# Backbone kernel: who loads the adaptive tiles, the bank of the context's mean, and where the last adaptive group is computed

## The chip, the cores and the metric

One core of a Trainium2 chip. The metric is device time in microseconds of one execution. Lower is better. The time before is 1668.27 us, the median of three runs (1666.53 to 1669.26).

## The reference, cut to what matters

Two layers over 512 latent tokens (x) and 256 context tokens (ctx) of width 1024, all float32. Layer 0 mixes tokens with a Conformer convolution, layer 1 with retention. Each is followed by a gated FFN of inner width 2816 with a three-tap convolution on the gate, and every sub-layer is modulated by an adaptive vector:

```python
mod_x = (silu_c @ ada_w[i] + ada_b[i])     # 6*1024 columns: shift, scale, gate (mixer); shift, scale, gate (FFN)
mod_c = (silu_cc @ ada_w[i] + ada_b[i])    # the same for the context
hx = modulate(rmsnorm(x, norm1_g[i]), sx1, cx1)
z = hx @ pw1_w + pw1_b                     # conv_module, for x and for ctx
u = dwconv(a * sigmoid(g), dw_w, dw_b)     # 31 taps over the tokens
u = silu(layernorm(u, ln_g, ln_b))         # mean and variance over the 1024 features
x = x + gx1 * (u @ pw2_w + pw2_b)
x = x + gx2 * conv_ffn(modulate(rmsnorm(x, norm2_g[i]), sx2, cx2), ...)
```

In layer 0 the context goes through the same steps with mod_c. The gate gx2 (and gc2) of layer 0 is the last sixth of the adaptive vector, and it is needed only when the FFN's output is added to x.

## The kernel before, in words

Features lie on the 128 partitions, in KT = 8 tiles, tokens along the free axis (LAT = 512, then CTX = 256, TOK = 768). Each engine has a program of its own, and semaphores order them. Every large product is three matmuls over parts rounded to fp32r: ScalarE writes w_hi (split_hi), VectorE w_lo (split_lo), and TensorE multiplies hi by hi, lo by hi and hi by lo. Weights come in units of 128 columns (512 KB) through a ring of RING = 4 buffers. SyncE's load waits until VectorE has split the unit four before (lo_ready).

Order of the stages: a first block (norm, adaptive groups 0 to 3, first units), PW1 with the depthwise convolution block by block, LayerNorm (named norm 1), PW2, FFN0, retention, FFN1, output.

The adaptive vector of layer 0 comes in 12 groups of four tiles of 128 columns. For group m, ada_products(m) streams 2 MB of weights through TensorE against silu(c) and silu(c_ctx), which stand in a 32-column stationary tile, into PSUM bank 6. ada_copy(m) on ScalarE copies the bank, ada_transposes(m) on TensorE transposes it into bank 7, and ada_sum(m) on VectorE adds four partial rows into mod. modulation(...) then adds the bias. SyncE loads groups 5 to 11 (load_group). Groups 10 and 11 lie in PW2.

The adaptive vector of layer 1 is 48 tiles of [128 columns, 1024 features]. GpSimd issues a load per job (L661) into two buffers mod_tile, and VectorE multiplies by the row silu(c) or silu(c_ctx) and sums along the row, one tensor_tensor_reduce per job (mod_jobs, L2160). MOD_JOBS holds 64 jobs, the first 16 tiles twice (c and c_ctx). They are spread over slots 1 to 20 of FFN0. A slot is one pass of VectorE over a feature block; it does some of its jobs ahead of the convolution's taps and the last two behind the products. A load for a buffer waits until the job that used it before is done (mod_job).

The convolution of a block: VectorE forms both_phases and the sum and even taps, TensorE seeds the even taps (first_evens, PSUM bank 4), ScalarE and GpSimd do the odd ones. For the last block TensorE also does ten taps (last_taps, banks 1 and 5), and VectorE ends the rows itself (last_rows). LayerNorm's means are matmuls of conv tiles with the constant matrix mean_of, float32. Two records each stand for one such matmul in the trace. Per tile j there is one for the latents (bank 0) and one for the context (bank 2). TensorE's order there is ada_products(8), first_evens, the mean of tile 0, last_taps, transposes 8, tiles 1 to 6, ada_products(9), tile 7. mu_summed then releases ScalarE and VectorE (center). variance(t) sums the squares of part t (parts 0 and 1 are latents, part 2 the context, 256 tokens each), root and recip make the inverse deviation, and norm_scale, SiLU, norm_hi and norm_lo write H_hi and H_lo of that part.

PW2 runs part by part, four units each. Its first two units of a part go feature by feature (by_rows), each waiting for H_lo of that feature. variance(2) and eight small products (mean_of with itself) follow the second unit of part 1.

Of the kernel before, what the change touches and what calls it, by code (L numbers as in the profile page):

```python
# [29 lines left out]
P = 128  # L30
D = 1024
# [98 lines left out]
MOD_TILES = 48  # L130
MOD_BUFS = 2
MOD_JOBS = [(j, v) for j in range(2 * KT) for v in range(2)] + [(j, 0) for j in range(2 * KT, MOD_TILES)]
# [8 lines left out]
def backbone(nc, x_cols, params, ada_groups, ada_cols, c_rows, w_units, decay_f, decay_b, gn_f, gn_b, eye, ages, tri_low, tri_up, rope_row, rope_col, token_cols, out_cols_major, out):  # L141
    with ExitStack() as stack:
# [158 lines left out]
        sum_part, odd_part = ps[:, 1, 0:HALF], ps[:, 5, 0:HALF]  # L301
# [203 lines left out]

        block = stack.enter_context(nc.Block())
# [12 lines left out]
        def _(sp):  # L519
# [42 lines left out]
            for b in range(KT + 2):  # L562
                load(2 * b + 4, (2 * b + 4) % RING)
                load(2 * b + 5, (2 * b + 5) % RING)
                if b < 6:
                    if b % 2 == 0:
                        load_group(b // 2 + 5)
                else:
                    load_group(b + 2)
            load_ffn(FFN0)  # L570
# [15 lines left out]
        def _(pool):  # L586
# [71 lines left out]
            for n, (j, _) in enumerate(MOD_JOBS):  # L658
                if n >= MOD_BUFS:
                    pool.wait_ge(mod_job, n - MOD_BUFS + 1)  # L660
                pool.dma_start(mod_tile[:, n % MOD_BUFS, :], ada_cols[j]).then_inc(mod_tile_in[n % MOD_BUFS], 16)  # L661
# [18 lines left out]
        def _(pe):  # L680
# [286 lines left out]

            ada_products(8)
            first_evens(PE_EVEN[1], 7 * (KT // 2), 1, S_PW1 // 2 + KT)
            slot_free(S_LN, None)  # L970
            for j in range(KT):
                if j == 1:
                    last_taps(KT - 1)
                    ada_transposes(8)
                if j == KT - 1:
                    ada_products(9)

                pe.wait_ge(conv_ready, j + 1)
                mm(slot(0, 0), mean_of[:], conv[:, j, 0:LAT], j == 0, j == KT - 1)
                m = mm(slot(0, 2)[:, 0:CTX], mean_of[:], conv[:, j, CTX_OUT:OUTW], j == 0, j == KT - 1)  # L980
# [31 lines left out]
            for t in range(3):  # L1012
                for i in range(4):
# [11 lines left out]
                    if n in (3, 5):  # L1025
                        ada_transposes(10 + t)
                    if n == 3:
                        ada_products(11)
# [166 lines left out]
        def _(act):  # L1195
# [171 lines left out]
            A(rstd[:, part(2)], bank(0, 2)[:, 0:PART], ACT.Copy).then_inc(slot_read[1], 1)  # L1367
# [147 lines left out]
            def ln_steps(t, i):  # L1515

                if (t, i) == (1, 0):
                    root(1, 2)
                if t < 2:
                    norm_hi(1, t + 1, LN_TILES[i])  # L1520
                if (t, i) == (0, 3):
                    ada_copy(11)
# [4 lines left out]
            def ffn(blk, s, layer, both, x_at):  # L1527
                f = 0
                for c_no, n in enumerate(CHUNKS):
# [32 lines left out]
                    blk, s = blk + n, s + n  # L1562
                    if c_no < len(CHUNKS) - 1:
                        out_phase(blk, s, x_at, both, layer, 40)
                    elif layer == DEPTH - 1:
                        last_out_phase(blk, s, x_at)
                    else:
                        out_phase_norm(blk, s, x_at, both, layer, 40, 3 + 2 * layer)
# [84 lines left out]
        def _(dve):  # L1653
# [473 lines left out]
            def ln_after(t, i):  # L2127
# [11 lines left out]
                if (t, i) == (1, 1):  # L2139
                    ada_sum(11, 0, 11)  # L2140
                    modulation(11, 0, 40, 48, 12)

            by_parts(2 * PW2, 0, S_PW2, 0, 0, 3, 2, ln_before, ln_after)
            dve.wait_ge(mod_ready, 13)
# [5 lines left out]
            def mod_jobs(slot, early):  # L2150

                first = len(MOD_JOBS) * (slot - 1) // MOD_SLOTS
                end = min(len(MOD_JOBS), len(MOD_JOBS) * slot // MOD_SLOTS)
                cut = max(first, end - MOD_BUFS)
                for n in range(first, cut) if early else range(cut, end):
# [5 lines left out]
                                           accum_out=mod[:, 1, j, c:c + 1]).then_inc(mod_job, 1)  # L2161

            def ffn(blk, s, layer, both, x_at):
# [5 lines left out]
                for c_no, n in enumerate(CHUNKS):  # L2169
                    def pairs(i):  # L2170
                        for q in range(2):
# [28 lines left out]
                            if both and f + 2 * i + q:  # L2200
                                mod_jobs(f + 2 * i + q, False)
                    if both:
# [195 lines left out]
def laid_out(inputs):  # L2398
# [24 lines left out]
    tiles = np.ascontiguousarray(w[1].T).reshape(MOD_TILES, P, D)  # L2423
# [80 lines left out]
```

## Time and profile before

| | |
|---|---|
| median of three runs | 1668.27 us (1666.53 to 1669.26) |
| the profiled execution | 1666.69 us, its span 1664.9 us |
| TensorE busy | 1642.7 us, 99% |
| VectorE busy | 1020.7 us, 61% |
| ScalarE, GpSimd busy | 669.9 us, 199.4 us |
| granted TensorE clock, mean | 0.998 |
| moved by DMA | 175.21 MB |

The span runs from the first to the last instruction. Start times below are us from its start. PE is TensorE, PEld its weight load, DVE VectorE, ACT ScalarE, POOL GpSimd, SP SyncE. L682 is line 682 of the kernel; helpers record all of their calls under one line, so the tiles tell which step a row is: all matmuls stand at L682, transposes of the adaptive groups at L877. A bracket with an arrow names what ended the idle time before the row.

### The profile page before, as it was taken

Reading aid. Unit: us, or ns where it says so; the run is one execution under the profiler, and the core shown is the slowest. Engines: PE = TensorE matmul, PEld = TensorE weight load, DVE = VectorE, ACT = ScalarE, POOL = GpSimd, SP = SyncE. Lnnn points to the kernel's source line nnn. Section 1 sums busy time; section 2 is a strip of 40 time slices with the busy share of each in tenths; the row PEclk is TensorE's granted clock in tenths of the full one; section 3 lists DMA queues with packets and bytes.
Section 4 is the critical chain, followed back from the end, with each engine's and each line's share of the span. In section 5 each row is a group of like instructions: output and inputs, shape, how many; then the busy total and the mean of one; then the engine's idle time right before and its main releaser. Section 6 shows DMA issues by size and latency. Waiting matters only on the chain.

```text
span 1664.9 us, 25492 instructions
## 1 busy us (share of the span) xinstructions
PE 1642.7 (99%) x9978; PEld 1443.8 (87%) x9978; DVE 1020.7 (61%) x1605; ACT 669.9 (40%) x1017; POOL 199.4 (12%) x248
## 2 busy tenths in 40 slices
PE   9999999999999999999999999999999999999998
PEld 7877769998888888888899999999999888888887
DVE  6899987856535652466468665656566644443445
ACT  4655646543322322232344433324235433333333
POOL 1588821011001100001000000000000000000001
PEclk9999999999999999999999999999999999999999
DMA  9322322243425342344213121212112223322321
GB/s 386 133 102 102 138 106 74 64 162 115 154 77 187 141 164 76 101 152 174 79 39 105 52 83 40 81 39 83 51 51 90 89 95 108 101 92 85 101 89 51
DMA packets 46779, 175.21 MB, mean 105 GB/s; under 512 B 5760, under 2 KB 7040, under 8 KB 43616
## 3 DMA queue, kind: packets, MB, share of 16 engines
q1 hardware_dynamic: 34928, 126.38, 22.3%
q0 software_dynamic: 11760, 47.58, 8.3%
q8 instruction: 61, 1.00, 0.3%
q14 instruction: 30, 0.25, 0.0%
HBM read 171.85 MB, written 2.10 MB: 104 GB/s over the span
## 4 chain that ended last, share of the span: by engine, by line
PE 82%; DVE 14%; ACT 3%; issue 1%; DVEq 0%; POOL 0%; ACTq 0%; POOLq 0%
PE ps L682 82%; DVE ps L1844 3%; DVE ps L1862 2%; DVE w_lo L1664 2%; DVE rstd L1670 1%; DVE H_lo L1705 1%; DVE tmp L1693 1%; DVE sq L1693 0%; DVE rstd L1681 0%; ACT sq L1256 0%; DVE X L2021 0%; ACT tmp L1256 0%; ACT H_hi L1247 0%; DVE both_phases L1949 0%; DVE H_lo L1703 0%
## 5 line engine op out<-in xcount | busy, mean ns | idle before, releaser
L682 PE MATMUL ps<-H_hi,w_hi 128*128 128x512 f32 (+1 forms) x1712 | 584.2, 341 | 3.3 <-DVE H_lo L1703 2.2
L682 PE MATMUL ps<-H_lo,w_hi 128*128 128x512 f32 (+1 forms) x1712 | 578.4, 338 | 0.0
L682 PE MATMUL ps<-H_hi,w_lo 128*128 128x512 f32 (+1 forms) x1712 | 577.9, 338 | 0.0
L682 PEld LDWEIGHTS ps<-H_hi,w_hi 128*128 128x128 f32 x1712 | 324.6, 190 | 47.6 <-issue 8.5
L682 PEld LDWEIGHTS ps<-H_lo,w_hi 128*128 128x128 f32 x1712 | 324.6, 190 | 35.3
L682 PEld LDWEIGHTS ps<-H_hi,w_lo 128*128 128x128 f32 x1712 | 324.5, 190 | 35.2
L1664 DVE TENSOR_TENSOR w_lo<-w_raw,w_hi 128x1024 fp32r<-128x1024 f32 x208 | 252.1, 1232 | 99.8 <-ACT w_hi L1209 76.5
L682 PE MATMUL ps<-mid_hi,w_hi 128*128 128x512 f32 (+1 forms) x592 | 200.0, 338 | 0.5
L682 PE MATMUL ps<-mid_hi,w_lo 128*128 128x512 f32 (+1 forms) x592 | 198.7, 336 | 0.0
L682 PE MATMUL ps<-mid_lo,w_hi 128*128 128x512 f32 (+1 forms) x592 | 198.6, 335 | 0.0
L682 PE MATMUL ps<-w_hi,H_hi 128*128 128x256 f32 x512 | 145.1, 283 | 0.2 <-DVE w_lo L1664 0.2
L682 PE MATMUL ps<-w_hi,H_lo 128*128 128x256 f32 x512 | 144.9, 283 | 0.0
L682 PE MATMUL ps<-w_lo,H_hi 128*128 128x256 f32 x512 | 144.8, 283 | 0.0
L1209 ACT ACTIVATE w_hi<-w_raw 128x1024 fp32r<-128x1024 f32 x128 | 132.5, 1050 | 19.0 <-PE ps L682 18.1
L2184 DVE SCALAR_TENSOR_TENSOR tmp<-ps,par,tmp 128x511 f32<-128x511 f32 x66 | 41.6, 658 | 150.8 <-ACT tmp L1543 76.2
L1543 ACT ACTIVATE tmp<-ps,par 128x512 f32<-128x512 f32 x44 | 34.3, 778 | 238.9 <-PE ps L682 238.9
L682 PEld LDWEIGHTS ps<-mid_hi,w_hi 128*128 128x128 f32 x592 | 111.1, 188 | 15.6 <-ACT tmp L1387 2.4
L682 PEld LDWEIGHTS ps<-mid_hi,w_lo 128*128 128x128 f32 x592 | 111.1, 188 | 13.2
L682 PEld LDWEIGHTS ps<-mid_lo,w_hi 128*128 128x128 f32 x592 | 111.2, 188 | 13.1
L617 POOL TENSOR_TENSOR odd_row<-odd_row,prod 128x392 f32<-128x392 f32 x107 | 112.4, 1050 | 43.1 <-ACT prod L1310 29.1
L2016 DVE TENSOR_TENSOR X<-X,tmp 128x768 f32 (+3 forms) x44 | 35.7, 812 | 131.1 <-ACT tmp L1387 131.1
L682 PEld LDWEIGHTS ps<-w_hi,H_hi 128*128 128x128 f32 x512 | 98.2, 192 | 0.7 <-issue 0.4
(285 smaller groups left out, 2202.1 us busy)
## 6 DMA issues: line engine op xcount, KB each, us to landing
w_raw<-in_w_units SPq DMA_DIRECT2D x190, 512.0 KB, 3.6
mod_tile<-in_ada_cols POOLq DMA_DIRECT2D x64, 512.0 KB, 4.9
ada<-in_ada_groups SPq DMA_DIRECT2D x14, 1024.0 KB, 6.5
w_raw<-in_w_units SPq DMA_DIRECT2D x16, 384.0 KB, 4.5
ada<-in_ada_groups POOLq DMA_DIRECT2D x4, 1024.0 KB, 11.0
ada_more<-in_ada_groups POOLq DMA_DIRECT2D x4, 1024.0 KB, 13.8
X<-in_x_cols SPq DMA_DIRECT2D x4, 768.0 KB, 7.0
w_raw<-in_w_units POOLq DMA_DIRECT2D x2, 512.0 KB, 14.6
```

The lines of the kernel that those rows point to most:

```text
L617: nc.gpsimd.tensor_tensor(row, row, prod[:, at % PROD_RING, 0:HALF], ALU.add).then_inc(prod_added, 1)
L682: return nc.tensor.matmul(o, a, b, start=first, stop=last, skip_group_check=True)
L1209: A(w_hi[:, r, :], w_raw[:, r, :], ACT.Copy).then_inc(hi_ready, 1)
L1543: a = A(tmp[:, q, LATS], bank(q, 1), ACT.Identity, scale=w1, bias=b)
L1664: v.tensor_tensor(w_lo[:, r, :], w_raw[:, r, :], w_hi[:, r, :].bitcast(F32), ALU.subtract) \
L1670: v.reciprocal(rstd[:, part(t)], rstd[:, part(t)]).then_inc(rstd_ready, 1)
L1693: o = v.scalar_tensor_tensor(b, X[:, j, part(t)], gain[:, layer, half, j, m:m + 1], rstd[:, part(t)], ALU.mult, ALU.mult)
L1705: o = v.scalar_tensor_tensor(dst, b, shift(norm, t, j), hi, ALU.add, ALU.subtract)
L1844: v.scalar_tensor_tensor(sum_acc, frm, w, sum_acc, ALU.mult, ALU.add).then_inc(tap_done, 1)
L1862: v.scalar_tensor_tensor(even_acc, frm, even_weight(j, b), even_acc, ALU.mult, ALU.add).then_inc(tap_done, 1)
L2016: v.tensor_tensor(row, row, tmp[:, p, 0:w], ALU.add).then_inc(x_updated, 1)
L2184: v.scalar_tensor_tensor(t[:, t0 + 1:t0 + m], b[:, 0:m - 1], wt[0], t[:, t0 + 1:t0 + m], ALU.mult, ALU.add).then_inc(g_taps, 1)
```

## The change

The adaptive group 11 of layer 0 (the FFN's gate, its last four tiles) is no longer computed on TensorE. Its four tiles are put in front of layer 1's 48 as transposed tiles, and each gives two sums, so MOD_JOBS holds 72 jobs. Their results go to the last four tiles of mod of layer 0 (job_sum). load_group(11), ada_products(11), ada_copy(11), the transposes and ada_sum(11) go. modulation over tiles 40 to 48 moves from PW2 into the FFN slot where the eighth job is done, and ScalarE waits for it before the first output phase.

SyncE issues the tile loads: load_first_ffn replaces load_ffn(FFN0), unrolled, and puts the tiles of a slot behind the load of every second unit from the eighth of a chunk on. GpSimd no longer issues any of them.

The context's mean gets bank 5, and the last odd taps bank 2 instead. The context means of tiles 0 to 5 are computed behind ada_products(8), ahead of first_evens; tiles 6 and 7 stay with the latents'.

```diff
@@ constants @@
+GATE_TILES = 4
+MOD_TILES = GATE_TILES + 48
+MOD_PAIRS = GATE_TILES + 2 * KT
+MOD_JOBS = [(j, v) for j in range(MOD_PAIRS) for v in range(2)] + [(j, 0) for j in range(MOD_PAIRS, MOD_TILES)]
-        sum_part, odd_part = ps[:, 1, 0:HALF], ps[:, 5, 0:HALF]
+        sum_part, odd_part = ps[:, 1, 0:HALF], ps[:, 2, 0:HALF]
+        def job_sum(j, c):
+            return mod[:, 0, 48 - GATE_TILES + j, c:c + 1] if j < GATE_TILES else mod[:, 1, j - GATE_TILES, c:c + 1]
+        def jobs_done(slot):
+            return min(len(MOD_JOBS), len(MOD_JOBS) * slot // MOD_SLOTS)
@@ SyncE @@
-                else:
+                elif b <= KT:
                     load_group(b + 2)
-            load_ffn(FFN0)
+            def load_tile(n):
+                if n >= MOD_BUFS:
+                    sp.wait_ge(mod_job, n - MOD_BUFS + 1)
+                sp.dma_start(mod_tile[:, n % MOD_BUFS, :], ada_cols[MOD_JOBS[n][0]]).then_inc(mod_tile_in[n % MOD_BUFS], 16)
+            def load_first_ffn():
+                first, slot, tile = 2 * FFN0, 0, 0
+                for n in CHUNKS:
+                    for u in range(2 * n + KT):
+                        load(first + u, (first + u) % RING, KT if u < 2 * n else n)
+                        if u >= KT and u % 2 == 0 and u < KT + 2 * n:
+                            if slot == 0:
+                                sp.wait_ge(h_lo_ready, KT * PARTS_BEFORE[3])
+                            while tile < min(len(MOD_JOBS), jobs_done(slot) + MOD_BUFS):
+                                load_tile(tile)
+                                tile += 1
+                            slot += 1
+                    first += 2 * n + KT
+            load_first_ffn()
@@ GpSimd @@
-            for n, (j, _) in enumerate(MOD_JOBS):
-                if n >= MOD_BUFS:
-                    pool.wait_ge(mod_job, n - MOD_BUFS + 1)
-                pool.dma_start(mod_tile[:, n % MOD_BUFS, :], ada_cols[j]).then_inc(mod_tile_in[n % MOD_BUFS], 16)
@@ TensorE @@
+            def mean_ctx(j):
+                pe.wait_ge(conv_ready, j + 1)
+                return mm(ps[:, 5, 0:CTX], mean_of[:], conv[:, j, CTX_OUT:OUTW], j == 0, j == KT - 1)
             ada_products(8)
+            pe.wait_ge(sig_ready, KT)
+            for j in range(KT - 2):
+                mean_ctx(j)
             first_evens(PE_EVEN[1], 7 * (KT // 2), 1, S_PW1 // 2 + KT)
...
                 mm(slot(0, 0), mean_of[:], conv[:, j, 0:LAT], j == 0, j == KT - 1)
-                m = mm(slot(0, 2)[:, 0:CTX], mean_of[:], conv[:, j, CTX_OUT:OUTW], j == 0, j == KT - 1)
+                if j >= KT - 2:
+                    m = mean_ctx(j)
...
-                    if n in (3, 5):
-                        ada_transposes(10 + t)
                     if n == 3:
-                        ada_products(11)
+                        ada_transposes(10)
@@ ScalarE @@
-            A(rstd[:, part(2)], bank(0, 2)[:, 0:PART], ACT.Copy).then_inc(slot_read[1], 1)
+            A(rstd[:, part(2)], ps[:, 5, 0:CTX], ACT.Copy).then_inc(slot_read[1], 1)
-                if (t, i) == (0, 3):
-                    ada_copy(11)
+                    if both and c_no == 0:
+                        act.wait_ge(mod_ready, 13)
@@ VectorE @@
-                if (t, i) == (1, 1):
-                    ada_sum(11, 0, 11)
-                    modulation(11, 0, 40, 48, 12)
-            dve.wait_ge(mod_ready, 13)
+            dve.wait_ge(mod_ready, 12)
-                first = len(MOD_JOBS) * (slot - 1) // MOD_SLOTS
-                end = min(len(MOD_JOBS), len(MOD_JOBS) * slot // MOD_SLOTS)
+                first, end = jobs_done(slot - 1), jobs_done(slot)
-                                           accum_out=mod[:, 1, j, c:c + 1]).then_inc(mod_job, 1)
+                                           accum_out=job_sum(j, c)).then_inc(mod_job, 1)
                                 mod_jobs(f + 2 * i + q, False)
+                                if jobs_done(f + 2 * i + q - 1) < 2 * GATE_TILES <= jobs_done(f + 2 * i + q):
+                                    dve.wait_ge(mod_job, 2 * GATE_TILES)
+                                    modulation(10, 0, 40, 48, 12)
@@ host @@
-    tiles = np.ascontiguousarray(w[1].T).reshape(MOD_TILES, P, D)
+    tiles = np.concatenate([w[0][:, (48 - GATE_TILES) * P:].T, w[1].T]).reshape(MOD_TILES, P, D)
```

## Rows read from the trace of the kernel before

**Rows 1.** The page's busy times: us (share of the span) xinstructions, by engine

```profile
PE 1642.7 (99%) x9978; PEld 1443.8 (87%) x9978; DVE 1020.7 (61%) x1605; ACT 669.9 (40%) x1017; POOL 199.4 (12%) x248
```

**Rows 2.** The waits of TensorE, 0 to 420 us: us in total, times, longest us

```profile
PE ps L682 <- DVE sq L1944: 4.5, 3, 2.3
PE ps L682 <- DVE H_lo L1703: 2.2, 2, 2.0
```

**Rows 3.** Timeline of TensorE, 199 to 228 us: start us, us, what xrecords [idle before]

```profile
199.60 1.47 PE L682 MATMUL ps<-ada,silu_c 128*32 128x512 f32 x12
203.42 4.57 PE L682 MATMUL ps<-sq,even_diag 128*128 128x393 f32 x8 [2.35 <-DVE sq L1944]
...
216.14 7.91 PE L682 MATMUL ps<-conv,mean_of 128*128 128x512 f32 x24
223.97 1.92 PE L682 MATMUL ps<-ada,silu_c 128*32 128x512 f32 x16
225.83 1.56 PE L682 MATMUL ps<-conv,mean_of 128*128 128x512 f32 x4
```

**Rows 4.** Timeline of TensorE, the even taps of an earlier block

```profile
161.29 2.88 PE L682 MATMUL ps<-sq,even_diag 128*128 128x393 f32 x8 [1.08 <-DVE sq L1944]
```

**Rows 5.** Busy time of a stretch: length, PE, PEld, DVE, ACT, POOL, granted clock, DMA, GB/s

```profile
204.00:207.40 3.40, 3.40 (x6) 1.69 (x6) 2.25 (x5) 3.40 (x8) 3.11 (x4) 0.50 0.99 417
```

**Rows 6.** Timeline of VectorE, 206 to 233 us

```profile
206.18 0.18 DVE L1722 TENSOR_REDUCE mod<-ps 128x8 f32<-128x32 f32 x1
208.03 0.63 DVE L1908 SCALAR_TENSOR_TENSOR ps<-sq,par,ps 128x393 f32<-128x393 f32 x1 [1.67 <-PE ps L682]
...
221.66 0.57 DVE L1979 TENSOR_TENSOR conv<-tap_sum,odd_row 128x392 f32<-128x392 f32 x1
...
227.42 5.39 DVE L1991 TENSOR_TENSOR conv<-conv,ps 128x256 f32<-128x256 f32 x16 [3.76 <-PE ps L682]
```

**Rows 7.** Timelines of GpSimd (sixth tile) and ScalarE (last gate)

```profile
182.31 1.09 POOL L631 TENSOR_TENSOR conv<-tap_sum,odd_row 128x392 f32<-128x392 f32 x1
...
191.06 0.47 ACT L1326 ACTIVATE rstd<-ps,par 128x256 f32<-128x256 f32 x1
```

**Rows 8.** Busy time of the stretch before PW2, columns as in rows 5

```profile
236.00:239.00 3.00, 1.37 (x16) 0.16 (x8) 0.23 (x1) 2.97 (x6) 0.00 (x0) 1.00 0.00 0
```

**Rows 9.** Timeline of TensorE in PW2, 251 to 277 us

```profile
251.95 1.06 PE L682 MATMUL ps<-ada,silu_c 128*32 128x512 f32 x8
253.95 1.07 PE L682 MATMUL ps<-ada,silu_c 128*32 128x512 f32 x8 [0.94 <-DMA ada<-in_ada_groups]
...
264.26 0.60 PE L877 MATMUL ps<-ident,ada_row 128*128 128x128 f32 x4
...
276.90 0.35 PE L682 MATMUL ps<-H_hi,w_hi 128*128 128x256 f32 x1 [0.19 <-DVE H_lo L1703]
```

**Rows 10.** Timelines of GpSimd and of VectorE in PW2

```profile
259.10 3.05 POOL L642 TENSOR_TENSOR prod<-conv 128x256 f32<-128x256 f32 x4
...
273.67 0.18 DVE L1722 TENSOR_REDUCE mod<-ps 128x8 f32<-128x32 f32 x1
...
274.10 0.42 DVE L1681 TENSOR_TENSOR rstd<-rstd,sq 128x256 f32<-128x256 f32 x1
...
276.33 0.76 DVE L1703 TENSOR_TENSOR H_lo<-sq,H_hi 128x256 fp32r<-128x256 f32 x2 [0.80 <-ACT H_hi L1247]
```

**Rows 11.** FFN: busy time of one pair (columns as rows 5), and the sums' line

```profile
407.01:423.62 16.61, 16.61 (x97) 14.70 (x96) 11.20 (x17) 4.94 (x6) 1.97 (x4) 1.00 0.44 143
...
L2160 DVE CUSTOM_DVE_ANT_0 mod_tile<-mod_tile,sq x48: 1216/1220/1227, 355.4 to 799.5; 128x1024 f32<-128x1024 f32 x48
```

**Rows 12.** FFN: timelines of SyncE and ScalarE, and a wait of VectorE

```profile
354.52 1.47 SPq L538 DMA_DIRECT2D w_raw<-in_w_units  x2
...
378.67 1.05 ACT L1218 ACTIVATE w_hi<-w_raw 128x1024 fp32r<-128x1024 f32 x1
...
DVE mod_tile L2160 <- DMA mod_tile<-in_ada_cols: 22.3, 21, 2.4
```

More of the change, by code:

```diff
@@ L129 @@
 PRODS = ODD_TAPS
-MOD_TILES = 48
+GATE_TILES = 4
+MOD_TILES = GATE_TILES + 48
 MOD_BUFS = 2
-MOD_JOBS = [(j, v) for j in range(2 * KT) for v in range(2)] + [(j, 0) for j in range(2 * KT, MOD_TILES)]
+MOD_PAIRS = GATE_TILES + 2 * KT
+MOD_JOBS = [(j, v) for j in range(MOD_PAIRS) for v in range(2)] + [(j, 0) for j in range(MOD_PAIRS, MOD_TILES)]
 MOD_SLOTS = FT - 2
```

## The prediction

> **What bounds the kernel now.** First the page's table of busy time: TensorE is busy 1642.7 of 1664.9 us [rows 1]. So a change is worth what it takes from TensorE's own work, or from one of its few waits, if TensorE or the engines beside it don't give it back. Then who TensorE waits for in the first 420 us, where the change lies: 4.5 us for VectorE's padded input (L1944), its longest wait 2.3 us, and 2.2 us for H_lo, the longest 2.0 us at 237.4 [rows 2, 8]. Both long ones sit between the depthwise convolution and its LayerNorm. So I read the timeline of TensorE there, and its granted clock, then VectorE's timeline beside it, and last the second pointwise product (PW2), where the last adaptive group is computed.
>
> **The convolution's end.** TensorE ends the products of group 8 at 201.07, stands 2.35 us until 203.42, then runs the first even taps of the last block: eight records in 4.57 us [rows 3]. The same eight took 2.88 us for an earlier block [rows 4]. The difference, 1.69 us, is the clock: from 204.0 to 207.4 it was granted at 0.50 of full, 1.2 instead of 2.4 GHz, after the sparse stretch before it [rows 5]. After the taps come the first mean, the last taps' products and transposes, from 216.14 to 223.97 the means of six tiles for latents and context, group 9's products (1.86 us), and from 225.83 the mean of the last tile [rows 3]. VectorE had finished the last row at 222.23 and starts to center only at 227.42, 3.76 us idle on TensorE [rows 6]. So from 208 to 227 TensorE's queue sets the end, with VectorE's chain as a near second: it waited 1.67 us for the slow even taps [rows 6].
>
> The change puts six of the eight context means ahead of these even taps. Both things they wait for are long there: the sixth convolution tile at 183.4, the last gate at 191.5 [rows 7]. Price of one: six pairs take 7.83 us [rows 3], a context mean has half the columns of a latent one, so a third of a pair: 7.83/18 = 0.43 us, six are 2.6 us. In the hole they run from 201.0 to 203.6, so the even taps start 0.1 to 0.2 us later than at 203.42, which is the least that this part can lose. In return TensorE has 2.6 us less to do behind the taps, and the sparse stretch is gone, so I take the taps at 2.88 us and not 4.57. Sum for the last mean: 2.6 + 1.7 - 0.1 = 4.2 us. Is VectorE late next? Its even taps start 1.5 us earlier (206.5 for 208.03), so the last row ends at 220.7; TensorE reaches the last mean at 225.83 - 4.2 = 221.6. TensorE still comes last, by 0.9 us. The new bank costs nothing: ScalarE has read the last gate out of bank 5 at 191.5 [rows 7], and bank 2 is free once the padded input is written, before the taps. Bounds for this step: 4.3 above; below, if the taps stay slow whatever is ahead of them, 4.2 - 1.7 = 2.5; if the fall also lands on the six means (their 2.6 become 5.2, the taps then full), the last mean gains 2.6 + 1.7 - 2.7 = 1.6.
>
> From there centering, variance, root, SiLU and the first H_lo follow as one chain without another source, and shift whole. The group 10 load is issued by group 9's products, and shifts too.
>
> The Trainium skill ("TensorE: Matmul & The Clock Gate", What's actually happening) says that the place of a clock change is free-running, not tied to the kernel's start. By that rule a hole of 2.35 us would be slow in some runs of before and not in others, and the second hole, 2.0 us at 237.4, at full clock here, would be slow in some; over such runs the step would be worth between 2.5 and 4.2. The row [rows 8] shows the second hole at 1.00 only in this execution.
>
> **The last group in PW2.** Gone from TensorE: the products from 251.95 to 255.0, 3.0 us with 0.94 of waiting for the load, and the transposes at 264.26, four records that overlap to 0.4 us: 3.4 us in all [rows 9]. I don't count this. ScalarE and VectorE hand the norm of the next part back and forth here and ask little of TensorE: with the products gone TensorE meets the variance squares, which GpSimd finishes at 262.15 [rows 10], and ends them at 262.6 for 264.26; and at 276.90 it already waits 0.19 us for the last H_lo of the context part [rows 9]. That H_lo comes at 276.33 from VectorE [rows 10], and TensorE can't pass it. What moves it is only what left VectorE's chain: the sum and the addition of group 11, 273.67 to 274.10, 0.43 us [rows 10]. So the part is worth 0.43 us; TensorE gets a new hole of about 1.6 us before that H_lo. Bounds: nothing, and 3.4 if the chain follows TensorE after all. ScalarE's copy of group 11 goes too, but it waits for VectorE's row at that place.
>
> **The FFN.** Eight more sums: 8 x 1.22 = 9.8 us of VectorE. In the pair of blocks with four sums VectorE is busy 11.2 of 16.6 us, TensorE 16.61 of 16.61 [rows 11]. TensorE never waits for VectorE there: cost nothing, because 5.4 us per pair are free and a pair gets 0.4 more sums, 0.5 us. If that cover failed, all 9.8 us would come. The one new addition to mod (0.17 us) and ScalarE's wait for it, before the first output phase, come two slots after the eighth sum; behind the wait stand ScalarE's weight splits, and the wait is met before.
>
> **The loads on SyncE.** 72 tiles for 64; one group of 2 MB goes. What is queued behind a tile load that waits for a sum: the next weight loads of the ring. But the next of these waits for a split that VectorE issues behind the same sums, so it would not have gone earlier. The cover if it did: a weight unit issued at 354.52 is first read by ScalarE at 378.67, 24 us later [rows 12]. Transfers are 512 KB, and the tile loads on GpSimd let VectorE wait 22.3 us in 21 places [rows 12], which TensorE doesn't see. So 0; below zero is excluded as TensorE has no wait there, above it by the 24 us. GpSimd's queue loses only what nobody behind waits for: its next load is for the retention.
>
> **The sum.** 4.2 + 0.43 = 4.65 us, 0.28%. The profiled execution took 1666.69 us (span 1664.9), and would be 1662.0; it lies 1.6 us under the median of 1668.27, which gives **1663.6 us** on the scale of the medians. 0.2% (3.3 us) is about what a measurement tells from no change.
>
> **Rivals.**
> A. The clock pays little: the even taps of before aren't slow in most runs, or the fall lands on the six means. Gain 2.0 (1.6 + 0.43) to 2.9 (2.5 + 0.43): 1665.4 to 1666.3. For it: one fall in one execution is all I have; against: the fall sits right behind the longest hole. Chance 0.25.
> B. PW2 follows TensorE: the whole 3.4 us counts. 1668.27 - 4.2 - 3.4 = 1660.6. For it: 3.0 us are TensorE's own; against: the wait at 276.90. Chance 0.08.
> C. The clock falls in the new hole of PW2, or in the one before it, where TensorE then has no slack. One fall costs 1.7 us (half of 3.4, [rows 5]), two 3.4: 1665.3 or 1667.0. For it: the new hole of 1.6 us; against: 2.0 us at 237.4 brought none [rows 8]. Chance 0.10.
> D. The other side: in the FFN VectorE's sums reach TensorE. One mechanism: the sums stand ahead of the convolution taps that free a PSUM slot. It decides once a pair's VectorE work passes 16.6 us for 11.2 now; its price is all eight sums, 9.8 us: 1668.27 - 4.65 + 9.8 = 1673.4. For it: the only thing added; against: 5.4 us free. Chance 0.07.
>
> Forecast 0.50. Faster by over 0.2% needs 3.3 us: most of the forecast (0.47), B, and little of A and C (0.02): 0.57. Slower is D: 0.07. Same: 0.36. Range: B at its low end 1660.5; A and single falls of C inside up to 1666.6; left out are D and the double fall, under 0.2. The forecast alone: 1662.5 to 1664.7.
>
> **What would show it.** Right: no hole at 201, clock 1.00 through the even taps in under 3 us, VectorE's wait before centering near 1 us for 3.76, with centering at 223.2; by_rows of the context part still ended by H_lo, its last record 4.6 us earlier, and a hole of 1 to 2 us before it; the FFN a copy of before with 3.6 sums a pair. Wrong: centering at 225 or later (A), no hole before the H_lo (B), half clock after 270 (C), a TensorE wait for VectorE between 337 and 820 (D).

## The result, and the profile after

The changed kernel takes 1659.51 us (median of 5 runs, 1659.09 to 1661.23), the kernel before 1668.27 us in the same rounds (1666.53 to 1671.43). The ratio is 0.9946, 95% interval 0.9933 to 0.9959: 8.8 us faster (6.8 to 11.2 by the interval), where 4.65 were forecast, and 1 us below the low end of the range. The profiled execution took 1661.17 us, its span is 1659.2. It lies 1.7 us above its median, where the one of before lay 1.6 below. So the two traces differ by 5.5 us in time (5.7 in span), and 3.2 us of the 8.8 are between the traces and the medians.

In the changed kernel helpers stand on other lines: matmuls at L709, transposes at L904, H_lo at L1737, the sums in the FFN at L2190. The page's busy times answer to [rows 1]:

```profile
PE 1640.7 (99%) x9958; PEld 1442.7 (87%) x9958; DVE 1030.1 (62%) x1620; ACT 669.1 (40%) x1016; POOL 165.8 (10%) x184
```

The timeline of TensorE at the end of the convolution answers to [rows 3]:

```profile
200.73 1.92 PE L709 MATMUL ps<-ada,silu_c 128*32 128x512 f32 x16
202.59 2.86 PE L709 MATMUL ps<-conv,mean_of 128*128 128x256 f32 x12
205.28 2.80 PE L709 MATMUL ps<-sq,even_diag 128*128 128x393 f32 x8
...
215.80 5.75 PE L709 MATMUL ps<-conv,mean_of 128*128 128x512 f32 x14
221.48 1.92 PE L709 MATMUL ps<-ada,silu_c 128*32 128x512 f32 x16
223.33 1.56 PE L709 MATMUL ps<-conv,mean_of 128*128 128x512 f32 x4
```

The hole of 2.35 us is gone, the six context means stand in it, and the even taps take 2.80 us for 4.57. Everything starts late, though: group 8's products ended 1.6 us earlier in the trace of before, and the first products on H_hi (30.43 us before, 32.05 now) were already as late. Two stretches of the changed kernel say why (length; busy us of PE, PEld, DVE, ACT, POOL; granted clock; DMA share; GB/s). The clock was 0.50 of full (1.2 GHz) near 20 us, where before had 1.00, and it is full (2.4 GHz) through the taps:

```profile
20.17:23.58 3.41, 3.10 (x8) 1.38 (x12) 0.39 (x3) 0.49 (x1) 0.00 (x0) 0.50 0.96 366
205.28:208.08 2.80, 2.80 (x10) 1.67 (x9) 2.58 (x5) 2.80 (x7) 2.58 (x4) 1.00 1.02 433
```

VectorE's timeline at the centering (answers to [rows 6], 3.76 us idle there):

```profile
221.75 0.57 DVE L2013 TENSOR_TENSOR conv<-tap_sum,odd_row 128x392 f32<-128x392 f32 x1
...
224.93 5.39 DVE L2025 TENSOR_TENSOR conv<-conv,ps 128x256 f32<-128x256 f32 x16 [1.17 <-PE ps L709]
```

From the end of group 8's products (201.07 before, 202.65 now) to the centering it was 26.35 us and is 22.28: 4.07 less. Read from the start of the span the centering stands at 224.93, just under the 225 that was to be the sign of case A; that sign took no account of a fall ahead of 201.

TensorE's three waits in PW2, and VectorE's row ahead of the last (answer to [rows 9, 10]):

```profile
254.57 0.36 PE L709 MATMUL ps<-H_hi,w_hi 128*128 128x256 f32 x1 [0.74 <-DVE H_lo L1737]
...
270.28 0.36 PE L709 MATMUL ps<-H_hi,w_hi 128*128 128x256 f32 x1 [0.18 <-DVE H_lo L1737]
...
273.98 0.35 PE L709 MATMUL ps<-H_hi,w_hi 128*128 128x256 f32 x1 [1.24 <-DVE H_lo L1737]
```

```profile
273.41 0.76 DVE L1737 TENSOR_TENSOR H_lo<-sq,H_hi 128x256 fp32r<-128x256 f32 x2 [0.80 <-ACT H_hi L1281]
```

The last H_lo came at 276.33 and comes at 273.41: 2.92 earlier, of which 2.49 were there at the centering (227.42 to 224.93), so PW2 gave 0.43. A pair of blocks in the FFN is the same 16.61 us with VectorE at 11.20 (answers to [rows 11]), and TensorE waits for nothing between 337 and 820:

```profile
404.09:420.70 16.61, 16.61 (x97) 14.70 (x96) 11.20 (x17) 4.94 (x6) 0.00 (x0) 1.00 0.50 170
```

The place that I had not read is the end. Line 142 before and 144 after is the program's closing; these rows are of the queues, not of the engines. Columns: queue, instruction, count, duration in ns (min/median/max), first and last start. Before:

```profile
L142 POOLq EVENT_SEMAPHORE  x2: 17/17/17, 1664.7 to 1664.8; - x2
L142 POOLq DRAIN  x1: 13994/13994/13994, 1650.7 to 1650.7; - x1
...
L142 SPq DRAIN  x1: 7/7/7, 1662.4 to 1662.4; - x1
L142 SPq EVENT_SEMAPHORE  x1: 17/17/17, 1664.8 to 1664.8; - x1
```

After:

```profile
L144 POOLq DRAIN  x1: 8762/8762/8762, 1647.2 to 1647.2; - x1
...
L144 SPq DRAIN  x1: 7/7/7, 1659.0 to 1659.0; - x1
```

The ledger of the two traces: +1.6 (the clock near 20 us), -4.07, -0.43, -2.25, and -0.5 left over, between 1265 and 1295 in the retention. That is -5.7. The profiled time of 1661.17 is close to the 1662.0 that the prediction gave for it, but by luck: 1.6 us of a fall that nobody forecast stand against 2.25 that nobody forecast either.

The 0.5 was not traced further. What stayed open after this was the 2.25, and the 3.2 between traces and medians.

### The profile page after: what moved, and what is told of

Read it like the earlier page. It is cut to its first block, busy times and chain, and to the rows that moved or that the text cites. A ratio compares the mean times of both kernels' runs of the same rounds, so it can differ in the third digit from the quotient of the medians.

```text
span 1659.2 us, 25253 instructions
## 1 busy us (share of the span) xinstructions
PE 1640.7 (99%) x9958; PEld 1442.7 (87%) x9958; DVE 1030.1 (62%) x1620; ACT 669.1 (40%) x1016; POOL 165.8 (10%) x184
## 3 DMA queue, kind: packets, MB, share of 16 engines
q0 software_dynamic: 2544, 14.03, 2.3%
## 4 chain that ended last, share of the span: by engine, by line
PE 85%; DVE 11%; ACT 3%; issue 1%; DVEq 0%; POOL 0%; ACTq 0%; POOLq 0%
PE ps L709 85%; DVE ps L1878 2%; DVE w_lo L1698 2%; DVE ps L1896 2%; DVE rstd L1704 1%; DVE H_lo L1739 1%; DVE tmp L1727 1%; DVE sq L1727 0%; DVE rstd L1715 0%; ACT sq L1290 0%; DVE X L2055 0%; ACT tmp L1290 0%; ACT H_hi L1281 0%; DVE H_lo L1737 0%; DVE conv L1835 0%
## 5 line engine op out<-in xcount | busy, mean ns | idle before, releaser
L709 PE MATMUL ps<-H_hi,w_hi 128*128 128x512 f32 (+1 forms) x1712 | 584.3, 341 | 5.2 <-DVE H_lo L1737 4.1
L709 PE MATMUL ps<-H_lo,w_hi 128*128 128x512 f32 (+1 forms) x1712 | 578.5, 338 | 0.0
L709 PE MATMUL ps<-H_hi,w_lo 128*128 128x512 f32 (+1 forms) x1712 | 577.8, 338 | 0.0
L709 PEld LDWEIGHTS ps<-H_hi,w_hi 128*128 128x128 f32 x1712 | 324.6, 190 | 49.1 <-issue 9.9
L709 PEld LDWEIGHTS ps<-H_lo,w_hi 128*128 128x128 f32 x1712 | 324.7, 190 | 35.5
L709 PEld LDWEIGHTS ps<-H_hi,w_lo 128*128 128x128 f32 x1712 | 324.4, 189 | 35.0
L709 PE MATMUL ps<-mid_hi,w_hi 128*128 128x512 f32 (+1 forms) x592 | 199.9, 338 | 0.5
L709 PE MATMUL ps<-mid_hi,w_lo 128*128 128x512 f32 (+1 forms) x592 | 198.7, 336 | 0.0
L709 PE MATMUL ps<-mid_lo,w_hi 128*128 128x512 f32 (+1 forms) x592 | 198.5, 335 | 0.0
L709 PE MATMUL ps<-w_hi,H_hi 128*128 128x256 f32 x512 | 145.2, 283 | 0.2 <-DVE w_lo L1698 0.2
L709 PE MATMUL ps<-w_hi,H_lo 128*128 128x256 f32 x512 | 144.9, 283 | 0.0
L709 PE MATMUL ps<-w_lo,H_hi 128*128 128x256 f32 x512 | 144.8, 283 | 0.0
L709 PEld LDWEIGHTS ps<-mid_hi,w_hi 128*128 128x128 f32 x592 | 111.1, 188 | 15.6 <-ACT tmp L1421 2.4
L709 PEld LDWEIGHTS ps<-mid_lo,w_hi 128*128 128x128 f32 x592 | 111.2, 188 | 13.1
L709 PEld LDWEIGHTS ps<-mid_hi,w_lo 128*128 128x128 f32 x592 | 111.1, 188 | 13.2
L709 PEld LDWEIGHTS ps<-w_hi,H_hi 128*128 128x128 f32 x512 | 98.2, 192 | 0.7 <-issue 0.4
```

The lines of the kernel that those rows point to most:

```text
L709: return nc.tensor.matmul(o, a, b, start=first, stop=last, skip_group_check=True)
```

## The experiments

Theory E (the end): every DMA that GpSimd issues lengthens its closing drain by about 0.08 us, and before it ended last. Theory L (late load): in the kernel before, SyncE's load of group 11 stands behind a weight load that waits for VectorE; it comes late by varying amounts, and a clock fall can follow the wait. Theory C (clock): the hole at 201 draws a fall (a fall is a stretch at half clock as in [rows 5], 1.7 us lost). The rivals are that the loads themselves, as traffic or as work of SyncE, make the difference, and that PW2 follows TensorE (B of the prediction).

"Before" was run with every group of kernels. Its medians were 1669.77 (29 runs, beside the first four), 1669.42 (23, beside the next four) and 1667.24 (11, beside the rest); each ratio is against the runs of before beside it. Between these groups the fastest run of before hardly moves (1664.46, 1664.30, 1664.65), the median by 2.5 us (the last group is from another chip); the changed kernel was run in its own rounds only, so medians set beside its 1659.51 come from other rounds.

**Only the loads on SyncE** (before, with 64 tile loads issued by SyncE).

```diff
-            load_ffn(FFN0)
+            load_first_ffn()
...
-            for n, (j, _) in enumerate(MOD_JOBS):
...
-                pool.dma_start(mod_tile[:, n % MOD_BUFS, :], ada_cols[j]).then_inc(mod_tile_in[n % MOD_BUFS], 16)
```

> The kernel before with one part of the change: SyncE issues the 64 tile loads, GpSimd none. Theory (drain): GpSimd's closing drain took 13.99 us before and 8.76 us after the change, with 72 loads fewer on it; before, it ended at 1664.7, 2.3 us behind SyncE's last work, and that end falls away. So the drain shortens to about 8.8 us and the time falls by 2.3 us, with nothing changed before the output. Rival (chance): the shorter tail of the changed kernel is scatter of the last stores, and the time stays within 0.5 us. The prediction had 0 for this part.

(The changed kernel's queue of GpSimd has 64 loads fewer than before, 89 to 25, and not 72 fewer.) 1666.82 us (1662.83 to 1669.61), ratio 0.9985 [0.9972, 0.9998], 3.0 us under before. Its closing rows:

```profile
L142 POOLq DRAIN  x1: 8784/8784/8784, 1650.6 to 1650.6; - x1
...
L142 SPq DRAIN  x1: 7/7/7, 1662.3 to 1662.3; - x1
```

The drain ends at 1659.3, SyncE at 1662.3: E holds in the rows, where the end moves by the 2.25. The times agree but are no measure of it: the interval runs from 0.3 to 4.7 us, and the fastest run is 1.6 under before's.

**Everything but the loads on SyncE** (the changed kernel, its 72 tile loads issued by GpSimd).

```diff
-            load_first_ffn()
+            load_ffn(FFN0)
...
+            for n, (j, _) in enumerate(MOD_JOBS):
...
+                pool.dma_start(mod_tile[:, n % MOD_BUFS, :], ada_cols[j]).then_inc(mod_tile_in[n % MOD_BUFS], 16)
```

> The changed kernel with all 72 tile loads back on GpSimd, the rest of the change kept. Theory (drain): drain about 14.6 us, the end 2.9 us later than the changed kernel's, so 5.9 us faster than before instead of 8.8. Rival (chance, or SyncE's loads help the FFN): if chance, 8.8 us faster than before; if the FFN, the loss shows between 337 and 820 us and not behind the last product.

1662.0 us (1661.66 to 1663.92), ratio 0.9952 [0.9935, 0.9969], 2.5 above the changed kernel's 1659.51 (other rounds; by the ratios it is 1.0, with intervals that overlap). All six of its runs lie above all five of the changed kernel. Rows of its end:

```profile
L144 POOLq DRAIN  x1: 14646/14646/14646, 1647.2 to 1647.2; - x1
...
L144 SPq DRAIN  x1: 7/7/7, 1659.0 to 1659.0; - x1
```

The drain is 0.65 us longer than before, for 8 more DMAs, and ends 2.9 us after SyncE, as expected. In this execution the clock was also at 0.50 from 237.7 on, in the second hole of the prediction's case C.

**Count or bytes** (the changed kernel, with 64 loads of 4 KB on GpSimd into an unused tile).

```diff
+        spare = sb("spare", [P, 8])
...
+            for n in range(64):
+                pool.dma_start(spare[:], params[:, 0:8]).then_inc(spare_in, 16)
+                pool.wait_ge(spare_in, 16 * (n + 1))
```

> The changed kernel with 64 small loads added on GpSimd in the first FFN (32 bytes for each partition, into a tile that nobody reads), one after the other. Theory (drain by count of loads): drain 8.76 + 64 x 0.082 = 14.0 us, 1661.2 us on the scale where the changed kernel has 1659.5, because the drain then ends 2.3 us behind SyncE's last work: 2 us slower than the changed kernel. Rival (drain by bytes moved): drain near 8.8 us and no change. Rival (chance): the same.

1656.46 us (1656.06 to 1660.34), ratio 0.9925 [0.991, 0.9941]. Rows of its end:

```profile
L144 POOLq DRAIN  x1: 14027/14027/14027, 1644.3 to 1644.3; - x1
...
L144 SPq DRAIN  x1: 7/7/7, 1656.1 to 1656.1; - x1
```

The drain is back at 14.03 us for 89 DMAs and ends 2.2 us after SyncE: it goes by their number, not by bytes. The kernel with the unused tile and no small loads (below) is 2.4 us faster than this one in the median (other rounds), about the price of that end. That the kernel is 3 us faster than the changed one nevertheless nobody expected; the unused tile was the suspect (below).

**Only the means** (before, with the new bank and the six context means ahead of the even taps).

```diff
-        sum_part, odd_part = ps[:, 1, 0:HALF], ps[:, 5, 0:HALF]
+        sum_part, odd_part = ps[:, 1, 0:HALF], ps[:, 2, 0:HALF]
...
+            for j in range(KT - 2):
+                mean_ctx(j)
             first_evens(PE_EVEN[1], 7 * (KT // 2), 1, S_PW1 // 2 + KT)
```

> The kernel before with one part of the change: the six context means ahead of the last block's even taps, in bank 5. Theory (hole and clock): between the products of group 8 and centering 4.1 to 4.2 us go, 2.5 of them by less work behind the taps and 1.7 by the clock staying at full, and the drain at the end is as before, so the time falls by 4.2 us where before had its fall of the clock at 204, by 2.5 us where it had not. GpSimd's drain is not on this path: it starts at its own last product, so the end moves with it. Rival (queue only): 2.5 us in every run.

1665.35 us (1662.03 to 1668.81), ratio 0.9972 [0.9958, 0.9986], 4.4 under before. The times fall into two groups, 5 runs at 1662.0 to 1662.6 and 7 from 1664.9 up. The profiled one (1667.5) shows why, TensorE's timeline and two stretches:

```profile
247.64 0.60 PE L877 MATMUL ps<-ident,ada_row 128*128 128x128 f32 x4
249.75 1.06 PE L682 MATMUL ps<-ada,silu_c 128*32 128x512 f32 x8 [1.51 <-DMA ada<-in_ada_groups]
252.31 1.94 PE L682 MATMUL ps<-ada,silu_c 128*32 128x512 f32 x8 [1.50 <-DMA ada<-in_ada_groups]
```

```profile
248.06:251.47 3.41, 1.24 (x10) 0.19 (x8) 2.58 (x8) 2.98 (x9) 0.00 (x0) 1.00 0.84 344
251.47:254.90 3.43, 2.59 (x11) 0.93 (x12) 2.64 (x8) 2.84 (x7) 1.03 (x2) 0.50 0.01 2
254.90:258.30 3.40, 3.40 (x18) 3.40 (x17) 3.40 (x5) 0.01 (x1) 3.40 (x5) 0.50 0.00 0
```

TensorE waits 3.0 us for group 11's load (0.94 in [rows 9]), and from 251.47 to 258.3 has half the clock. The centering was 3.8 us early here, and PW2 gave 4.6 back. The load was not issued late: it went out at 242.10, where before had 245.87, early like the centering; but its two transfers took 8.2 us in the median, for 6.6.

The fast group is 2.4 us under before's fastest run (1664.46): without a fall at 204 to remove, the step is worth the 2.5 us of its work alone, as I had expected for such runs.

**Only the last group on VectorE** (before, with 72 jobs; their loads stay on GpSimd).

```diff
-                    if n == 3:
-                        ada_products(11)
+                    if n == 3:
+                        ada_transposes(10)
...
+                                if jobs_done(f + 2 * i + q - 1) < 2 * GATE_TILES <= jobs_done(f + 2 * i + q):
```

> The kernel before with one part of the change: group 11 as eight sums of VectorE in the FFN, all 72 tile loads on GpSimd. Theory: TensorE's 3.4 us are not gained, only VectorE's 0.43 us, and eight more loads lengthen the drain by 8 x 0.08 = 0.65 us, which is exposed at the end: within 0.5 us of before, drain about 14.6 us. Rival (TensorE's work counts): 3.4 us faster. Rival (loads don't matter to the drain): 0.4 us faster with a drain of 14.0 us.

1666.76 us (1666.06 to 1670.32), ratio 0.9987 [0.9976, 0.9997], 3.0 under before. I expected nothing beyond 0.5. The fastest run is 1.6 us slower than before's 1664.46, of which the drain (0.66 longer) less the 0.43 of VectorE explains 0.2; the rest is about one fall, and the trace (1666.41) has the one at 204. But the upper times are rarer, 2 of 12 above 1669 for 16 of 29, as L has it. The 3.0 us could also be taken for B's 3.4. Against that, from the centering to the last H_lo the trace has 48.48 us for 48.91 before, 0.43 and no more. L now needed a test of its own.

**Only the order of SyncE's loads** (before, group 11 loaded ahead of weight units 22 and 23).

```diff
             for b in range(KT + 2):
+                if b == KT + 1:
+                    load_group(b + 2)
                 load(2 * b + 4, (2 * b + 4) % RING)
...
-                else:
+                elif b <= KT:
                     load_group(b + 2)
```

> The kernel before with one line moved: SyncE issues group 11's load ahead of the loads of weight units 22 and 23, and not behind them. Theory (late load): the load was issued at 245.9, because the one for unit 23 waits for VectorE's split at 244.3; TensorE then waited 0.9 us for it in before's profile and 3.0 us in that of e2_mean_bank, where the clock fell for 6.8 us right behind and PW2 took 4.6 us longer. Issued about 9 us earlier it is there in time: no wait of TensorE for a DMA near 252, no fall between 250 and 262, and of before's times those at 1670 and above go, so the median falls by 2 to 3 us, while the fastest times stay. Rival (falls come anyway from the 32-column products): the times above 1670 stay and the median moves by less than 1 us.

1666.2 us (1664.19 to 1667.01), ratio 0.998 [0.997, 0.9989]: 3.2 under before. The fastest run is as fast as before's (1664.3), and nothing is left above 1667.01, where before had 19 of 23. The products run without the wait:

```profile
251.18 0.60 PE L879 MATMUL ps<-ident,ada_row 128*128 128x128 f32 x4
251.71 1.92 PE L684 MATMUL ps<-ada,silu_c 128*32 128x512 f32 x16
```

So one line, out of its place in a queue, costs the kernel before 3 us in the median and nothing in its best runs. That the loss goes by the clock is read from the mean granted clock of each run:

```
mean clock   before: runs, us                    group 11 first: runs, us
0.995        7, 1669.4 to 1672.2 (med. 1670.8)   none
0.996        8, 1667.4 to 1671.9 (med. 1670.1)   none
0.997        5, 1666.6 to 1668.6 (med. 1667.5)   5, 1665.9 to 1667.0
0.998, 0.999 3, 1664.3 to 1667.2 (med. 1666.5)   7, 1664.2 to 1666.4
```

The columns are the runs of before beside this kernel, and its own. The mean counts falls only roughly: of the traces with a single fall at 204, that of before shows 0.998 and that of the kernel with only the last group on VectorE 0.997. The changed kernel's five runs all lie at 0.998 or 0.999. What no trace of before caught is the late load with its fall: of the five traces with this load in its old place the waits are 0.9, 0.9, 3.0, 0.2 and 0.6 us, and only behind the 3.0 (the means alone, above) stands half clock. That this is what the slow runs of before have is argued, not shown.

**Only the hole filled** (before, with six context means added ahead of the even taps; the eight behind stay, so nothing is taken off TensorE).

```diff
+            for j in range(KT - 2):
+                mean_ctx(j)
             first_evens(PE_EVEN[1], 7 * (KT // 2), 1, S_PW1 // 2 + KT)
```

> The kernel before with six context means computed a second time, into bank 5, ahead of the last block's even taps; nothing is taken away behind the taps. Theory (clock): the even taps run at full clock in under 3 us, the fall at 204 is gone and centering comes about 1.6 us earlier, so the times with that fall move by 1.6 us and those without by nothing: median 1 to 1.6 us faster. Rival (queue only): the six more products cost 0.1 us and bring nothing.

1665.15 us (1664.32 to 1668.3), ratio 0.9978 [0.9968, 0.9988], 4.3 under before in the median (I had expected 1 to 1.6), the fastest run equal. TensorE has 2.7 us more to do and the kernel is faster. Timeline and stretches:

```profile
201.18 2.86 PE L682 MATMUL ps<-conv,mean_of 128*128 128x256 f32 x12
203.88 2.80 PE L682 MATMUL ps<-sq,even_diag 128*128 128x393 f32 x8
```

```profile
203.40:206.90 3.50, 3.50 (x12) 2.11 (x12) 3.20 (x7) 3.36 (x7) 3.28 (x4) 1.00 1.01 424
238.49:241.90 3.41, 3.41 (x19) 3.41 (x18) 2.92 (x8) 3.41 (x10) 0.00 (x0) 0.50 0.00 0
```

The taps are at full clock; in this execution the fall came behind the second hole (2.0 us at 237), where [rows 8] showed none. All fourteen traces together say how firm C is. Five have the open hole at 201, and four of them half clock in the taps behind it (before, its second trace, the last group on VectorE, the order of the loads; not the loads on SyncE). Nine have it filled, and none of these has it. The second hole of 2.0 us stands in all, with half clock within 6 us behind it in three. A stretch at half clock near 20 us, where nothing was changed, is in six. So a hole draws a fall often, not always.

This kernel and the one with the means alone also give the worth of the work taken off: neither has a fall ahead of its centering, which starts at 226.12 here and at 223.65 there, 2.5 us apart.

**Load of TensorE in PW2** (the changed kernel, nine small products where group 11's were).

```diff
                         ada_transposes(10)
+                        for _ in range(9):
+                            mm(ps[:, 6, 0:P], mean_of[:], mean_of[:], True, True)
```

> The changed kernel with nine products of constant matrices (18 records, 1.9 us) put where group 11's products were, into the PSUM bank that they used. Theory (H_lo bounds PW2): TensorE had 0.74, 1.24 us and the squares' waits free behind this place, so PW2 ends where it does in the changed kernel: 0 us, at most 0.3. Rival (B, TensorE's work counts): 1.9 us slower.

1659.01 us (1658.82 to 1659.54), ratio 0.9949 [0.9933, 0.9964]. TensorE's timeline has 2.2 us more work and the same wait of 1.24 us at its end; B is refuted.

```profile
247.87 2.17 PE L709 MATMUL ps<-mean_of 128*128 128x128 f32 x18
...
272.49 0.36 PE L709 MATMUL ps<-H_hi,w_hi 128*128 128x256 f32 x1 [1.24 <-DVE H_lo L1739]
```

**Another order of groups 9 and 10** (the changed kernel, group 9's products behind variance(1), out of the means' way, group 10's in PW2).

```diff
-                if j == KT - 1:
-                    ada_products(9)
...
             variance(1)
-            ada_products(10)
+            ada_products(9)
...
                     if n == 3:
-                        ada_transposes(10)
+                        ada_transposes(9)
+                        ada_products(10)
```

> The changed kernel with group 9's products taken from ahead of the last mean to behind the variance of part 1, and group 10's from there to the place in PW2 that group 11's had before. Theory: the last mean, which TensorE reached at 223.33 while VectorE's last row ended at 222.32, starts 1.0 us earlier; the 2 us of group 9's products lie in the hole ahead of PW2, and group 10's, 2.3 us with their transposes, in the holes of PW2 that the change left (0.74 and 1.24 us and the squares' waits). 1.0 us faster than the changed kernel. Rival (PW2 is full): PW2 ends later by 1 us or more and the gain is gone.

1658.58 us (1657.99 to 1659.46), ratio 0.9937 [0.9921, 0.9952]: 0.9 under the changed kernel, which the medians alone (of different rounds) would not show; its trace and that of the kernel above, both without a fall, have spans of 1656.6 and 1657.5. After the change VectorE's chain is next (idle 1.17 us, I had said 0.9). Taking 1.9 us off TensorE there moves the wait: TensorE now waits 0.82 us for VectorE's last row.

```profile
220.36 1.56 PE L709 MATMUL ps<-conv,mean_of 128*128 128x512 f32 x4 [0.82 <-DVE conv L2013]
```

**The unused tile alone** (the changed kernel and one line; no instruction is added), and **the same with the order of groups above**.

```diff
+        spare = sb("spare", [P, 8])
```

> The changed kernel with an unused tile of 32 bytes for each partition put ahead of the phases' tiles, so that mid_hi, mid_lo and all tiles behind it lie 32 bytes further; nothing else. In e7_small_dmas, which has the same tile, the matmuls over mid_hi and mid_lo took 2.98 us less in sum (1776 records, some 229 to 232 ns from start to start instead of 231 to 235), and the kernel was 3 us faster than the changed one in spite of its longer drain. Theory (address): 2.9 us less TensorE time here too, drain 8.8 us, 5 us faster than e7_small_dmas' sum of a longer drain would have it: 1654.5 us where the changed kernel has 1659.5 (2.9 for the address gives 1656.6; the drain is not exposed in either). So 1656.6 us by the address alone. Rival (the small loads did it): 1659.5 us and 234 ns as in the changed kernel.

> The candidate: e9_products_later (group 9's and 10's products later) with the 32-byte tile of e12_pad. Theory: the two gains add, 1.0 and 2.9 us under the changed kernel, 1655.6 us. Rival: the address gain is one of the small loads, 1658.6 us.

1654.03 us (1653.62 to 1657.18), ratio 0.992 [0.9904, 0.9936], and 1654.43 us (1652.82 to 1655.23), ratio 0.9918 [0.9902, 0.9934]. These two are the fastest, and not told apart, where I had expected 1 us between them and 1656.6 for the tile alone. The tile takes 32 bytes per partition, so tiles behind it start 32 bytes further on. Groups of TensorE's instructions by form, out of the changed kernel (busy us, mean ns of one, idle before):

```profile
L709 PE MATMUL ps<-mid_hi,w_hi 128*128 128x512 f32 x288 | 114.4, 397 | 0.5
L709 PE MATMUL ps<-mid_lo,w_hi 128*128 128x512 f32 x288 | 113.8, 395 | 0.0
L709 PE MATMUL ps<-mid_hi,w_lo 128*128 128x512 f32 x288 | 113.8, 395 | 0.0
```

and with the unused tile:

```profile
L710 PE MATMUL ps<-mid_hi,w_hi 128*128 128x512 f32 x288 | 113.9, 396 | 0.6
L710 PE MATMUL ps<-mid_lo,w_hi 128*128 128x512 f32 x288 | 112.8, 392 | 0.0
L710 PE MATMUL ps<-mid_hi,w_lo 128*128 128x512 f32 x288 | 112.7, 391 | 0.0
```

From start to start, over all 1776 matmuls on mid_hi and mid_lo, that is 3.0 us (311.53 and 308.55), the same as with the small loads. The matmuls on H_hi and H_lo keep their time. In the medians it is 5.5 us against the changed kernel, and 5.0 against the kernel with nine products, run in the same rounds. The third kernel with the tile, with the other order of groups, has 306.08, which is 5.5 less. There the matmuls of 256 columns are faster too, which are 85.5 us and 281 ns in the changed kernel:

```profile
L710 PE MATMUL ps<-mid_hi,w_hi 128*128 128x256 f32 x304 | 84.7, 279 | 0.0
```

So the same shift is worth 3.0 us in two traces and 5.5 in one. The profiled execution of the tile alone is the slowest of its six (1657.18, the fastest 1653.62), and has no fall of the clock; whether the other five had the faster matmuls is not known. Why the address matters, and what decides between the two sizes, stays open.

**Before, one more look.**

> The kernel before once more, for its profile alone. Theory (late load): if this execution is above 1669 us, its profile has a wait of TensorE for group 11's load near 252 of over 1.3 us and a fall of the clock behind it; if it is at 1666.7 or less, a wait under 1.1 us and none. Rival: slow executions show the same wait and no fall there.

1668.77 us, between the two kinds that I had expected. The clock was at 0.50 three times, behind 20.6, 205.0 and 242.5, and the load was waited for 0.6 us only. So a slower run of before is not always the late load; here it was two more falls elsewhere, and this trace does not support L.

## Why the prediction was right in its parts and wrong in its sum

**The convolution's end: right.** Forecast 4.2 us, measured 4.07 between the same two points in the one pair of traces, with means, taps and VectorE's idle time as worked out (2.86 for 2.6, 2.80 for 2.88, 1.17 for 0.9). The clock's 1.7 us was the disputed term; the kernel with only the hole filled shows the taps at full clock. Of the 4.2 it is 1.7 that a run gains only if it had the fall: four of five traces had it, the fastest runs of before did not gain it (2.4 us with the means alone).

The Trainium skill ("TensorE: Matmul & The Clock Gate", What's actually happening) was weighed there: that the place of a clock change is free-running. The traces agree as far as they go: near 20 us (six of fourteen), at 204 (four of the five with the hole) and at 238 a fall is present in some executions of like code and absent in others.

**PW2: right.** 0.43 us forecast and measured; B refuted by the dummy products.

**The FFN: right.** No wait of TensorE, the pair the same 16.61 us; D did not occur.

**The loads on SyncE: this step failed.** It said "So 0; below zero is excluded as TensorE has no wait there", and "GpSimd's queue loses only what nobody behind waits for". I looked for who waits in the FFN, and not at the end of the program, where GpSimd's drain waits in proportion to all that the queue has issued. The term is -2.25 us, shown by the closing rows of both halves (the drain ends ahead of SyncE with the loads on SyncE, 2.9 us behind it with them on GpSimd) and by the 64 small loads; the medians of the halves, 3.0 and 2.5, agree. One look at what starts after the last output would have shown GpSimd's 13.99 us beside SyncE's 1662.4 in the trace of before.

**The step to the medians: failed too.** The sum was made on one execution at 0.998 and shifted by 1.6 us, as if the change left the scatter of clock falls alone. But it takes away two places where they arise, the hole at 201 and the load at 252. The fastest runs show the size. Before's fastest of 68 is 1664.30, the changed kernel's of five 1659.09: 5.2 us, and 2.5 (the work ahead of the centering) + 0.43 + 2.25 are 5.2, with no clock term. So in the medians the falls are worth 8.8 - 5.2 = 3.6 us, where the forecast had one, 1.7. The 4.1 us that it lacked are these 1.9 and the 2.25 of the end. Single parts show it: 4.3 us for filling the hole where the trace has 1.7, 3.2 us for the load's order where it has 0.94, at no gain in the fastest run. The 0.94 stood in [rows 9], and I costed the wait as part of TensorE's slack: right for that execution, not for one like that of the means alone, in which it is three times as long and half clock follows.

The parts nearly add up: in medians means -4.4 and last group -3.0 give -7.4, both together -7.8 (the kernel with the loads on GpSimd); the three ratios 0.9972, 0.9987 and 0.9985 give 0.9944 as a product, the changed kernel has 0.9946. How the falls divide between the two places stays open. Filling the hole takes 4.3 us and moving the load 3.2, but before's median is only 5.1 above its fastest run, so the two overlap; and the means alone gain no more (4.4) than the hole filled, though they take 2.5 us of work off besides.

## What to carry to other kernels

Read the trace to its last row: the program ends when the last queue is drained, and if that is GpSimd's, each DMA taken from it is worth its share of the drain, whoever waits for the data, until another queue ends last. If one profile lies well away from the median, look at the granted clock of all runs, and at each wait of TensorE that something variable ends (a load behind another engine's semaphore): its price can be a fall behind it, and not the wait. Move such a load ahead of the waiting one before changing any arithmetic.

## What the runs showed of the hardware that was not expected

- GpSimd's closing drain, counted from its last arithmetic, took 2.13 us for 25 DMAs issued and 7.35 for 89 (0.08 us for each); with 97 the whole record is 0.65 to 0.66 us longer than with 89. 64 loads of 4 KB weigh as much as 64 of 512 KB (14.03 and 13.99 us).
- An unused tile of 32 bytes per partition made 1776 matmuls 3.0 us faster in all in two traces and 5.5 in a third; in a stretch of 512-column ones the distance from start to start went from 234 to 229 ns. Which operand's place it is was not tried.
- A TensorE hole of 2 to 3 us draws a clock fall in some executions and not in others: the one at 201 in four of five traces, the one at 237 in three of fourteen; a kernel with 2.7 us more TensorE work in such a hole was faster, 0.9978 [0.9968, 0.9988].
